# Two-layer float32 transformer chain on one core: mLSTM heads scored in pairs with the engines' orders changed, and eight low halves of weights made by GpSimd

## The chip, the cores and the metric

One NeuronCore of a Trainium2 chip runs the whole program. TensorE (PE) multiplies, VectorE (DVE) and ScalarE (ACT) do elementwise work, GpSimd (POOL) does a little of it and issues some transfers, SyncE (SP) issues the weight transfers. The metric is the device time of one execution in microseconds (us), lower is better.

## The reference

Activations of 256 tokens by 1024 features pass through two blocks of two layers each, all in float32. The two places that the change touches are the latent attention of the first layer and the mLSTM mixer of the last one:

```python
def _mla(x, positions, w_dq, q_norm, w_uq, w_dkv, kv_norm, w_ukv, w_o):
    cq = _rmsnorm(x @ w_dq, q_norm)
    q = (cq @ w_uq).reshape(b, s, h, MLA_NOPE + MLA_ROPE)      # 8 heads, 128 + 64
    q = jnp.concatenate([q[..., :MLA_NOPE], _rope(q[..., MLA_NOPE:], ...)], axis=-1)
    ckv = x @ w_dkv
    c_kv = _rmsnorm(ckv[..., :MLA_KV_LORA], kv_norm)
    k_pe = _rope(ckv[..., None, MLA_KV_LORA:], ...)
    kv = (c_kv @ w_ukv).reshape(b, s, h, MLA_NOPE + MLA_V)
    ...                                                          # causal softmax attention
    return o.reshape(b, s, h * MLA_V) @ w_o

def mlstm_mixer(u, b_gates, qk_conv_w, head_norm_g):             # 4 heads of 192
    qk, v, o_pre, gates = jnp.split(u, [2 * D_TOK, 3 * D_TOK, 4 * D_TOK], -1)
    qk = jax.nn.silu(causal_dwconv(qk, qk_conv_w))
    q, k = jnp.split(qk, 2, -1)
    ...
    # per head: sc = (q @ k.T) * w_intra ; num = sc @ v + inter-chunk state
    # den = sum(sc) + ... ; h = num / max(|den|, exp(-m))
    h = (h - mu) * lax.rsqrt(var + LN_EPS) * head_norm_g
    return jax.nn.sigmoid(o_pre) * h

def second_block(...):
    ...
        u = x @ w_in_mlstm[j]
        tok = mlstm_mixer(u[..., :4 * D_TOK + 2 * ML_HEADS], ...)
        xa = memory_cross_attention(u[..., -D_XA:], mem_kv)
        mix = jnp.concatenate([tok, xa], -1) @ w_out[l]
```

## The kernel before

**Weights in units.** Every weight matrix is cut into units of up to 128 x 2048 numbers, listed in the order of use (`order`). SyncE loads them in that order into six slots; a unit's slot comes free when TensorE has finished with the unit six places earlier. Each float32 number is used as two parts: ScalarE copies the loaded unit (`raw`) into a high half (`whi`, `split_hi`, L288), and a subtraction makes the low half (`wlo<-raw,whi`). VectorE makes the low half (`split_lo`, L299), in three cases GpSimd (`split_lo_gpsimd`, L293). TensorE then multiplies three times (`product`, L438): high by high, high by low, low by high. Before it uses a unit it waits for its low half (`wait_split`).

**Order by hand.** Each engine runs one list of instructions in the order written; nothing is reordered, and the engines meet only in semaphores. A `Splitter` makes the splits of all units in turn: `split.after(u)` makes those up to four units beyond u. Where such a call stands in an engine's list decides when that unit's half is made, and what waits behind it.

**Latent attention** (`mla_tensor`, `mla_scalar`, `mla_vector`, the first 78 us). Its units are numbered 0 to 12: 0 to 3 down projections, 4 to 6 the query projections (4 the rotary part `qp`, 5 and 6 the heads, `qn0` and `qn1`), 7 and 8 the key and value projections (`kn`, `v`), 9 to 12 the output projection. VectorE turns the rotary parts (`rotate`, L1223 to L1228) and normalises the latents (`roots`, a chain of small instructions at L424 to L430), then makes four low halves in a row (`split.after(qn1, 5)`: units 8 to 11), then the attention's maxima and divisions. TensorE transposes the normalised latents (`turn_latents`) before it can start on unit 6.

**mLSTM** (`ml_tensor`, `ml_scalar`, `ml_vector`, 1228 to 1368 us). Units: `VG` 0 to 3 (values and gates), `XQ` 4, `QK` 5 to 10 (queries and keys, two chunks of 128 channels each), `OU` 11 to 14 (output gate), `WO` 15 to 18 (output projection). A QK unit goes through TensorE (`qk_unit`), a first tap and a tanh on ScalarE, three taps and a gate on VectorE (`taps` L2244, `gate` L2260). Four heads of 192 channels lie over chunks of 128, so a head is one whole chunk and one half of another. `score(h)` (L2037) multiplies keys with queries, `masked` and `weights` make the decay weights, `weighted` (L2278) multiplies them in, `numerator` (L2053 to L2057) multiplies with the values, `divided` divides. `maxima` (L2025) spreads a row of maxima over the partitions. `cross1` is the cross attention to the memory, in steps between the others (L1676, L490, L1700). At the end VectorE normalises the heads and makes the tokens (`l_tok`), which TensorE transposes (`turn_tokens`) between pieces of `WO[0]`; `WO[1]` to `WO[3]` follow in `tail_tensor`.

Of the kernel before, what the change touches and what calls it, by code (L numbers as in the profile page):

```python
# [26 lines left out]
P = 128  # L27
# [21 lines left out]
def build(nc, a, out):  # L49
# [29 lines left out]
    with ctx:  # L79
# [286 lines left out]

        first_loaded = sem("first_loaded")
# [1584 lines left out]
        def num_bank(h):  # L1952
            return (3, 4, 5, 4)[h]

        def score_bank(h):
            return (7, 7, 7, 6)[h]

        def qk_needed(h):

            return (2, 4, 6, 6)[h]  # L1960
# [22 lines left out]
        def ml_tensor(pe):  # L1983
# [36 lines left out]
            def maxima(h):  # L2020
                if h < 2:
                    pe.wait_ge(L["l_gc"], 2)
                else:
                    pe.wait_ge(L["l_wd"], 2)
# [3 lines left out]
            def score(h):  # L2028
                pe.wait_ge(L["l_qkd"], qk_needed(h))
                if h in (1, 2):  # L2030
                    pe.wait_ge(L["l_scd"], h)
                if h == 3:
                    pe.wait_ge(L["l_wd"], 4)
                pieces = head_rows(h)
                for to, k0, q0 in ((slice(0, S), 0, 0), (slice(S, 3 * P), P, P)):
                    for n, (c, r) in enumerate(pieces):
                        m = nc.tensor.matmul(ps[:, score_bank(h), to], l_qk(TC + c)[r, 0, k0:k0 + P],  # L2037
                                             l_qk(c)[r, 0, q0:S], start=n == 0,
                                             stop=n == len(pieces) - 1, skip_group_check=True)
                m.then_inc(L["l_sT"], 1)  # L2040

            def numerator(h):
                pe.wait_ge(L["l_scd"], h + 1)
                if h == 1:
                    pe.wait_ge(L["l_conv"], TC)
                if h == 2:
                    pe.wait_ge(L["l_conv"], TC)
                if h == 3:
                    pe.wait_ge(L["l_hd"], 2)
# [38 lines left out]
            qk_unit(2)  # L2088
            maxima(0)
            maxima(1)  # L2090
            cross1.tensor(pe, 2)
            qk_unit(3)
            score(0)
            cross1.tensor(pe, 3)
            qk_unit(4)
            numerator(0)
            cross1.tensor(pe, 4)
            qk_unit(5, (0,))
            qk_unit(5, (1,))
            score(1)  # L2100
            maxima(2)
            pe.wait_ge(L["l_wd"], 2)
            maxima(3)
            for j, u in enumerate(OU):
                wait_split(pe, u)
                for t in range(TT):
                    if j == 0 and t == 0:
                        pe.wait_ge(cross1.low, cross1.PAIRS)
                    if j == 0 and t == 1:
                        pe.wait_ge(L["l_hd"], 1)  # L2110
# [3 lines left out]
                    if j == 2 and t == 0:  # L2114
                        numerator(2)
                        numerator(3)
                m.then_inc(w_done[u.slot], 1)
                if j == 0:
                    numerator(1)
                if j == 1:  # L2120
                    score(2)
                    score(3)
# [19 lines left out]
        def ml_scalar(act, link, split):  # L2142
# [55 lines left out]
            act.wait_ge(L["l_gc"], 2)  # L2198
            weights(0)
            weights(1)  # L2200
            first_tap(3)
            cross1.scalar(act, 3)
            tanh(2)
            split.after(QK[3])
            first_tap(4)
            cross1.scalar(act, 4)
            tanh(3)
            split.after(QK[4])
            tanh(4)
            first_tap(5)  # L2210
            weights(2)
            tanh(5)
            split.after(QK[5])
            weights(3)
# [22 lines left out]
        def ml_vector(dve, link, split):  # L2237
# [106 lines left out]
            split.after(QK[1])  # L2344
            cross1.vector(dve, link, 2)
            masked(0)
            masked(1)
            taps(2)
            gate(1)
            split.after(QK[2])  # L2350
            cross1.vector(dve, link, 3)
            weighted(0)
            taps(3)
            gate(2)
            cross1.vector(dve, link, 4)
            split.after(QK[3])
            taps(4)
            gate(3)
            divided(0)
            split.after(QK[4])  # L2360
            gate(4)
            taps(5)
            weighted(1)
            masked(2)
            masked(3)
            head_stats(0)
            gate(5)
            split.after(QK[5])
            divided(1)
# [317 lines left out]
```

## Time and profile before

| what | value |
|---|---|
| median of 3 runs | 1559.56 us (1559.52 to 1561.84) |
| profiled execution | 1563.72 us, its span 1561.9 us, mean granted TensorE clock 0.996 |
| TensorE matmul busy | 1546.5 us, 99% |
| VectorE, ScalarE, GpSimd busy | 1051.3, 770.1, 35.6 us |

The span is what the profiler saw between first and last instruction; the profiled execution's own time is 1.8 us more. Matmuls are pipelined and their ends modelled, so a busy TensorE can also be a slow one: the granted clock of a stretch must be read beside it.

### The profile page before, as it was taken

What the parts mean: (1) busy time and instruction counts of PE and PEld (TensorE: products, weight loads), DVE (VectorE), ACT (ScalarE), POOL (GpSimd) and SP (SyncE); (2) the same over time, 40 slices, a digit from 0 to 9 for tenths busy, and PEclk for the clock granted to TensorE, in tenths of its full rate; (3) what the DMA queues carried; (4) which work ended last, traced back from release to release, by engine and by line L of the source; (5) the groups of instructions that cost most, each with busy time, mean ns of one, the idle gap of its engine ahead of it and who ended that gap; (6) DMA issues with size and microseconds to landing.
All of it is one profiled execution on the core that took longest, in us unless ns stands there. A gap on an engine that the chain in (4) does not pass through costs nothing.

```text
span 1561.9 us, 20701 instructions
## 1 busy us (share of the span) xinstructions
PE 1546.5 (99%) x8610; PEld 1338.4 (86%) x8610; DVE 1051.3 (67%) x1270; ACT 770.1 (49%) x913; POOL 35.6 (2%) x86
## 2 busy tenths in 40 slices
PE   9999999999999999999999999999999999999997
PEld 9888888899888888888899888888888897888886
DVE  7866657768676666655777665576555877965556
ACT  5735434567353444545464354545445464454543
POOL 2000000000000000000100000010000100000000
PEclk9999999999999999999999999999999998999999
DMA  9365654743565656555463755547555562375551
GB/s 286 121 215 189 190 189 161 242 162 109 170 209 191 192 182 216 188 189 190 162 214 135 242 189 188 189 156 246 192 189 188 161 208 84 126 243 189 189 190 53
DMA packets 198356, 285.97 MB, mean 183 GB/s; under 512 B 9199, under 2 KB 166967, under 8 KB 198263
## 3 DMA queue, kind: packets, MB, share of 16 engines
q1 hardware_dynamic: 194663, 272.19, 53.3%
q0 software_dynamic: 3456, 11.94, 2.4%
q8 instruction: 68, 1.11, 0.3%
q10 hardware_dynamic: 144, 0.52, 0.1%
q14 instruction: 25, 0.20, 0.0%
HBM read 283.58 MB, written 1.05 MB: 182 GB/s over the span
## 4 chain that ended last, share of the span: by engine, by line
PE 95%; DVE 3%; ACT 1%; issue 1%; DMA 0%; DVEq 0%; ACTq 0%
PE ps L438 50%; PE ps L467 25%; PE ps L471 13%; PE ps L490 3%; DVE wlo L299 1%; PE ps L2037 1%; ACT whi L288 0%; PE ps L1456 0%; DVE arena L2244 0%; PE ps L1700 0%; DMA x<-in_x 0%; DVE x L566 0%; PE ps L1131 0%; PE ps L1123 0%; PE ps L1121 0%
## 5 line engine op out<-in xcount | busy, mean ns | idle before, releaser
L299 DVE TENSOR_TENSOR wlo<-raw,whi 128x2048 fp32r<-128x2048 f32 (+3 forms) x254 | 567.1, 2262 | 222.2 <-ACT whi L288 221.5
L288 ACT ACTIVATE whi<-raw 128x2048 fp32r<-128x2048 f32 (+3 forms) x260 | 480.3, 1884 | 19.2 <-DMA raw<-in_w_out 5.1
L438 PE MATMUL ps<-whi,yt 128*128 128x512 f32 (+1 forms) x1472 | 460.8, 386 | 0.5 <-DVE wlo L299 0.5
L467 PE MATMUL ps<-xt,whi 128*128 128x512 f32 x1728 | 432.3, 392 | 0.0
L467 PEld LDWEIGHTS ps<-xt,whi 128*128 128x128 f32 x1728 | 314.2, 189 | 59.0
L438 PEld LDWEIGHTS ps<-whi,yt 128*128 128x128 f32 x1472 | 274.8, 188 | 54.5 <-DVE wlo L299 0.9
L438 PE MATMUL ps<-wlo,yt 128*128 128x512 f32 (+1 forms) x736 | 283.8, 386 | 0.0
L471 PEld LDWEIGHTS ps<-xt,wlo 128*128 128x128 f32 x1728 | 235.7, 190 | 16.9
L471 PE MATMUL ps<-xt,wlo 128*128 128x256 f32 x1728 | 240.9, 282 | 0.0
L438 PE MATMUL ps<-whi,xt 128*128 128x512 f32 (+4 forms) x778 | 220.2, 361 | 0.9 <-DVE wlo L299 0.3
L777 ACT ACTIVATE arena<-ps 128x512 f32<-128x512 f32 x108 | 64.2, 594 | 279.8 <-PE ps L471 279.8
L438 PEld LDWEIGHTS ps<-whi,xt 128*128 128x128 f32 x778 | 140.3, 190 | 22.6 <-issue 1.6
L438 PEld LDWEIGHTS ps<-wlo,yt 128*128 128x128 f32 x736 | 138.6, 188 | 24.6
L810 DVE TENSOR_TENSOR arena<-arena,ps 128x512 f32<-128x512 f32 x108 | 73.9, 684 | 125.4 <-ACT arena L777 125.4
L438 PE MATMUL ps<-wlo,xt 128*128 128x512 f32 (+4 forms) x389 | 138.5, 356 | 0.0
L800 ACT ACTIVATE yt<-arena 128x512 fp32r<-128x512 f32 x76 | 48.2, 634 | 124.4 <-DVE arena L830 69.4
L438 PE MATMUL ps<-xt,whi 128*128 128x256 f32 x560 | 102.7, 285 | 0.3 <-DVE wlo L299 0.3
L438 PEld LDWEIGHTS ps<-xt,whi 128*128 128x128 f32 x560 | 87.3, 192 | 4.0 <-issue 3.4
L840 DVE TENSOR_TENSOR yt<-arena,yt 128x512 fp32r<-128x512 f32 x76 | 52.6, 693 | 53.2 <-ACT yt L800 53.2
L438 PEld LDWEIGHTS ps<-wlo,xt 128*128 128x128 f32 x389 | 73.9, 190 | 9.2
L438 PE MATMUL ps<-xt,wlo 128*128 128x256 f32 x280 | 79.2, 283 | 0.0
L525 ACT ACTIVATE xt<-ps 128x512 fp32r<-128x512 f32 x40 | 22.7, 597 | 90.5 <-PE ps L490 90.5
(248 smaller groups left out, 943.2 us busy)
## 6 DMA issues: line engine op xcount, KB each, us to landing
raw<-in_ffn_w_up SPq DMA_DIRECT2D x76, 1024.0 KB, 5.3
raw<-in_ffn_w_down SPq DMA_DIRECT2D x76, 1024.0 KB, 4.8
raw<-in_ffn_w_gate SPq DMA_DIRECT2D x44, 1024.0 KB, 5.3
raw<-in_diff_w_qkv SPq DMA_DIRECT2D x12, 1024.0 KB, 5.1
raw<-in_w_in_conv SPq DMA_DIRECT2D x10, 1024.0 KB, 5.2
raw<-in_w_out SPq DMA_DIRECT2D x8, 1024.0 KB, 4.8
raw<-in_w_in_mlstm SPq DMA_DIRECT2D x7, 1024.0 KB, 8.3
raw<-in_w_in_mlstm SPq DMA_DIRECT2D x8, 768.0 KB, 4.2
```

The source lines that it names most:

```text
L288: nc.scalar.activation(whi[:, u.slot, 0:u.size], raw[:, u.slot, 0:u.size], ACT.Copy).then_inc(w_hi[u.slot], 1)
L299: nc.vector.tensor_tensor(wlo[:, u.slot, 0:u.size], raw[:, u.slot, 0:u.size], whi[:, u.slot, 0:u.size].bitcast(F32), ALU.subtract).then_in ...
L438: m = nc.tensor.matmul(out_, p, q, start=first and n == 0, stop=last and n == 2, skip_group_check=True)
L467: nc.tensor.matmul(o.rearrange("p (a n) -> p a n", a=2), parts[c][0], xt2[:, :, c, :], start=c == 0, stop=False, skip_group_check=True)
L471: m = nc.tensor.matmul(o[:, S:2 * S], parts[c][1], xthi[:, c, :], start=False, stop=c == KC - 1, skip_group_check=True)
L490: return nc.tensor.transpose(o, i, ident[0:i.shape[0], 0:i.shape[0]])
L525: nc.scalar.activation(half_x(xthi, t, h), turn_view(n, t, h), ACT.Copy).then_inc(x_hi, 1)
L777: nc.scalar.activation(f_half(kind == "U" and f.gated), both_halves(f_bank(f, kind, s), 1), ACT.Copy).then_inc(f_part, 1)
L800: nc.scalar.activation(h_part(s, 0), f_view(1), ACT.Copy).then_inc(f_hi, 1)
L810: nc.vector.tensor_tensor(f_half(2 + (kind == "U" and f.gated)), f_half(kind == "U" and f.gated), both_halves(f_bank(f, kind, s), 0), ALU. ...
L840: nc.vector.tensor_tensor(h_part(s, 1), f_view(1), h_part(s, 0).bitcast(F32), ALU.subtract).then_inc(f_lo, 1)
L2037: m = nc.tensor.matmul(ps[:, score_bank(h), to], l_qk(TC + c)[r, 0, k0:k0 + P], l_qk(c)[r, 0, q0:S], start=n == 0, stop=n == len(pieces) - ...
```

## The change

In the mLSTM stage, heads are scored two at a time (`scores(h)` for heads h and h + 1 into two banks). The whole chunk of the first head comes first, then the two halves of the shared chunk, alternating between the heads, then the whole chunk of the second. The two pairs now stand within unit `QK[5]` and within `OU[1]`; all engines' lists are rearranged around that, some banks change, and the mask products stand between halves of other units. VectorE makes no low half for eight units; GpSimd makes them: units 4, 6, 9, 10, 11, 12 of latent attention, and `WO[1]` and `WO[2]` of mLSTM.

```diff
         def split_lo(dve, u):
+            if u in pool_low:
+                return
             dve.wait_ge(w_hi[u.slot], u.use)
...
+        pool_low = [mla_u[k] for k in (4, 6, 9, 10, 11, 12)] + [ml_u[k] for k in (16, 17)]
...
         def num_bank(h):
-            return (3, 4, 5, 4)[h]
+            return (5, 4, 5, 4)[h]
         def score_bank(h):
-            return (7, 7, 7, 6)[h]
+            return 7 - h % 2
...
-            def score(h):
+            def scores(h):
                 pe.wait_ge(L["l_qkd"], qk_needed(h))
-                if h in (1, 2):
-                    pe.wait_ge(L["l_scd"], h)
-                if h == 3:
-                    pe.wait_ge(L["l_wd"], 4)
-                pieces = head_rows(h)
-                for to, k0, q0 in ((slice(0, S), 0, 0), (slice(S, 3 * P), P, P)):
-                    for n, (c, r) in enumerate(pieces):
-                        m = nc.tensor.matmul(ps[:, score_bank(h), to], l_qk(TC + c)[r, 0, k0:k0 + P],
-                                             l_qk(c)[r, 0, q0:S], start=n == 0,
-                                             stop=n == len(pieces) - 1, skip_group_check=True)
+                pe.wait_ge(L["l_wd"], h + 2)
+                if h:
+                    pe.wait_ge(L["l_scd"], 1)
+                (whole0, shared0), (shared1, whole1) = head_rows(h), head_rows(h + 1)
+                spans = ((slice(0, S), 0, 0), (slice(S, 3 * P), P, P))
+                def piece(g, part, span, first):
+                    (c, r), (to, k0, q0) = part, span
+                    return nc.tensor.matmul(ps[:, score_bank(g), to], l_qk(TC + c)[r, 0, k0:k0 + P],
+                                            l_qk(c)[r, 0, q0:S], start=first and span is spans[0],
+                                            stop=not first, skip_group_check=True)
+                for span in spans:
+                    piece(h, whole0, span, True)
+                for span in spans:
+                    m = piece(h, shared0, span, False)
+                    piece(h + 1, shared1, span, True)
+                m.then_inc(L["l_sT"], 1)
+                for span in spans:
+                    m = piece(h + 1, whole1, span, False)
                 m.then_inc(L["l_sT"], 1)
...
         def _(pool):
             start_gpsimd(pool)
+            for k in (4, 6):
+                split_lo_gpsimd(pool, mla_u[k])
             wait_high(pool, mla_u[8])
             load_gb(pool, 0)
+            for k in (9, 10, 11, 12):
+                split_lo_gpsimd(pool, mla_u[k])
             pool.wait_ge(m_ylo, KC)
...
+                    for k in (16, 17):
+                        split_lo_gpsimd(pool, ml_u[k])
```

**GpSimd in latent attention.** In the list of GpSimd before, these rows follow the making of the constants (`gb` takes a layer norm's gains and shifts, the row with `in_mem` the memory tokens):

```order
L2444 AFFINE_SELECT mtril<-mtril 128x128
L2446 AFFINE_SELECT sel<-sel 4x512
L594 DMA gb<-in_ln_mix_g 128x1024 [waits w_hi2]
L594 DMA gb<-in_ln_mix_b 128x1024
L2612 DMA arena<-in_mem 128x2x1024 [waits m_ylo]
L594 DMA gb<-in_ln_ffn_g 128x1024 [waits ln_x]
```

In the changed kernel the same place reads:

```order
L2454 AFFINE_SELECT sel<-sel 4x512
L293 TENSOR_TENSOR wlo<-raw,whi 128x1536 [waits w_hi4]
L293 TENSOR_TENSOR wlo<-raw,whi 128x1536 [waits w_hi0]
L597 DMA gb<-in_ln_mix_g 128x1024 [waits w_hi2]
L597 DMA gb<-in_ln_mix_b 128x1024
L293 TENSOR_TENSOR wlo<-raw,whi 128x2048 [waits w_hi3]
L293 TENSOR_TENSOR wlo<-raw,whi 128x2048 [waits w_hi4]
L293 TENSOR_TENSOR wlo<-raw,whi 128x2048 [waits w_hi5]
L293 TENSOR_TENSOR wlo<-raw,whi 128x2048 [waits w_hi0]
L2624 DMA arena<-in_mem 128x2x1024 [waits m_ylo]
```

Six subtractions now stand here, for units 4 and 6 ahead of the first gains and for units 9 to 12 behind them, each waiting only for its high half.

**VectorE in latent attention.** This is VectorE's list before, from the end of the rotation of the queries (second half of the tokens) to the first maxima of the attention:

```order
L1227 TENSOR_TENSOR res<-ps,rope_m 128x512
L1228 TENSOR_TENSOR res<-res,arena 128x512 [waits dve_step]
L299 TENSOR_TENSOR wlo<-raw,whi 128x2048 [waits w_hi2,m_qpe]
L299 TENSOR_TENSOR wlo<-raw,whi 128x2048 [waits w_hi3]
L299 TENSOR_TENSOR wlo<-raw,whi 128x2048 [waits w_hi4]
L299 TENSOR_TENSOR wlo<-raw,whi 128x2048 [waits w_hi5]
L1286 COPY arena<-ps 128x512 [waits m_v0] x2
L936 TENSOR_TENSOR ps<-ps,masks 128x256 [waits mla_scored]
L940 TENSOR_REDUCE small<-ps 128x1 [waits dve_step]
```

In the changed kernel it reads:

```order
L1230 TENSOR_TENSOR res<-ps,rope_m 128x512
L1231 TENSOR_TENSOR res<-res,arena 128x512 [waits dve_step]
L301 TENSOR_TENSOR wlo<-raw,whi 128x2048 [waits w_hi2,m_qpe]
L1289 COPY arena<-ps 128x512 [waits m_v0] x2
L939 TENSOR_TENSOR ps<-ps,masks 128x256 [waits mla_scored]
L943 TENSOR_REDUCE small<-ps 128x1 [waits dve_step]
```

Of the four low halves in a row only that of unit 8 is left, between an addition with two operands in SBUF and the copies of the values; the low half of unit 6 is gone from a place 11 rows further up.

**TensorE in mLSTM.** Before, from unit `QK[3]` to `QK[4]` (`ps<-yf` is a score, `ps<-ident,arena` and `ps<-arena,kvm` the cross attention, `128x193` a numerator; the "..." stands for the unit's other products):

```order
L438 MATMUL ps<-xt,whi 128x256 [waits l_conv,w_lo2]
...
L2037 MATMUL ps<-yf 128x256 [waits l_qkd]
L2037 MATMUL ps<-yf 128x256
L2037 MATMUL ps<-yf 128x128 x2
L490 MATMUL ps<-ident,arena 128x128 [waits cross1_copied,cross1_normed]
L1700 MATMUL ps<-arena,kvm 64x256 [waits cross1_exped,cross1_copied]
L438 MATMUL ps<-xt,whi 128x256 [waits l_conv,w_lo3]
...
L2053 MATMUL ps<-arena 128x193 [waits l_scd]
L1700 MATMUL ps<-arena,kvm 64x256 [waits cross1_copied]
```

In the changed kernel, from `QK[3]` to the scores within `QK[5]`:

```order
L441 MATMUL ps<-xt,whi 128x256 [waits l_conv,w_lo2]
...
L493 MATMUL ps<-ident,arena 128x128 [waits cross1_copied,cross1_normed]
L1703 MATMUL ps<-arena,kvm 64x256 [waits cross1_exped,cross1_copied]
L441 MATMUL ps<-xt,whi 128x256 [waits l_conv,w_lo3]
...
L1703 MATMUL ps<-arena,kvm 64x256 [waits cross1_copied]
L441 MATMUL ps<-xt,whi 128x256 [waits l_conv,w_lo4]
...
L2041 MATMUL ps<-yf 128x256 [waits l_wd,l_qkd]
L2041 MATMUL ps<-yf 128x128
L2041 MATMUL ps<-yf 128x256 x2
L2041 MATMUL ps<-yf 128x128 x2
```

No score stands behind `QK[3]` any more; the first pair comes after the first half of `QK[5]`, and nothing between asks for `l_qkd` or `l_scd`, which VectorE's gates and weighted scores raise.

## Rows read from the trace of the kernel before

**Rows 1.** TensorE's waits, whole kernel: us in total, times, longest us.

```profile
PE ps L2037 <- DVE yf L2260: 2.3, 1, 2.3
...
PE ps L438 <- DVE wlo L299: 1.0, 3, 0.5
```

**Rows 2.** A window of mLSTM: length, PE busy, PEclk, DMA share, GB/s.

```profile
1295.30:1302.10 6.80, 6.80 (x25) 0.51 0.16 63
```

**Rows 3.** Timeline of TensorE, mLSTM: start, us, what [idle before].

```profile
1294.93 3.33 PE L2037 MATMUL ps<-yf 128*128 128x256 f32 x8 [2.27 <-DVE yf L2260]
...
1316.00 2.16 PE L2037 MATMUL ps<-yf 64*128 64x256 f32 x8
...
1330.15 3.74 PE L2037 MATMUL ps<-yf 128*128 128x256 f32 x16
```

**Rows 4.** The chain that ended last, mLSTM: start, us, what.

```profile
1319.22 5.92 PE ps L438 x24
...
1326.12 4.20 PE ps L438 x24
```

**Rows 5.** Windows of latent attention: columns as in the window above.

```profile
57.00:62.00 5.00, 4.40 (x33) 1.00 0.68 210
71.00:79.00 8.00, 7.32 (x40) 1.00 0.01 2
```

**Rows 6.** Timeline of GpSimd: its first low half, end of a feed-forward stage.

```profile
769.25 4.91 POOL L293 TENSOR_TENSOR wlo<-raw,whi 128x2048 fp32r<-128x2048 f32 x1 [168.01 <-ACT whi L288]
```

**Rows 7.** Timeline of VectorE around the GpSimd row above.

```profile
767.40 2.29 DVE L299 TENSOR_TENSOR wlo<-raw,whi 128x2048 fp32r<-128x2048 f32 x1 [1.18 <-ACT whi L288]
769.61 0.68 DVE L541 SCALAR_TENSOR_TENSOR res<-x,ps 128x512 f32<-128x512 f32 x1
...
772.73 1.99 DVE L559 SCALAR_TENSOR_TENSOR res<-res,mv,gb 128x512 f32<-128x512 f32 x1
...
776.01 0.75 DVE L559 SCALAR_TENSOR_TENSOR res<-res,mv,gb 128x512 f32<-128x512 f32 x1
```

**Rows 8.** The same at GpSimd's second low half: GpSimd, then VectorE.

```profile
1043.18 4.91 POOL L293 TENSOR_TENSOR wlo<-raw,whi 128x2048 fp32r<-128x2048 f32 x1 [168.05 <-ACT whi L288]
...
1046.65 1.98 DVE L559 SCALAR_TENSOR_TENSOR res<-res,mv,gb 128x512 f32<-128x512 f32 x1
```

**Rows 9.** Timeline of VectorE in latent attention.

```profile
29.47 0.19 DVE L2573 TENSOR_SCALAR rope_m<-ang 128x64 f32<-128x64 f32 x1
...
35.09 1.75 DVE L299 TENSOR_TENSOR wlo<-raw,whi 128x1536 fp32r<-128x1536 f32 x1
...
42.24 0.69 DVE L1228 TENSOR_TENSOR res<-res,arena 128x512 f32<-128x512 f32 x1
...
45.14 8.90 DVE L299 TENSOR_TENSOR wlo<-raw,whi 128x2048 fp32r<-128x2048 f32 x4
```

**Rows 10.** Timeline of ScalarE in latent attention: the high halves.

```profile
27.56 3.55 ACT L288 ACTIVATE whi<-raw 128x1536 fp32r<-128x1536 f32 x2
...
37.97 3.75 ACT L288 ACTIVATE whi<-raw 128x2048 fp32r<-128x2048 f32 x2
...
42.53 3.76 ACT L288 ACTIVATE whi<-raw 128x2048 fp32r<-128x2048 f32 x2
```

**Rows 11.** Timeline of TensorE: the starts of units 6 and 8.

```profile
36.89 0.50 PE L438 MATMUL ps<-xt,whi 128*128 128x256 f32 x2 [0.25 <-DVE wlo L299]
...
47.49 0.50 PE L438 MATMUL ps<-whi,xt 128*128 128x512 f32 x1 [0.27 <-DVE wlo L299]
```

**Rows 12.** Timeline of ScalarE, end of mLSTM: high halves of WO[0] to WO[2].

```profile
1326.51 5.50 ACT L288 ACTIVATE whi<-raw 128x2048 fp32r<-128x2048 f32 x3
```

**Rows 13.** Timeline, end of mLSTM: VectorE's third division to first tokens.

```profile
1337.01 0.16 DVE L2287 COPY small<-ps 128x2 f32<-128x2 f32 x1 [0.32 <-PE ps L2057]
...
1346.39 0.96 DVE L2398 SCALAR_TENSOR_TENSOR res<-res,arena 128x768 f32<-128x768 f32 x1
```

**Rows 14.** Timeline of TensorE: the transposes of the first tokens.

```profile
1348.29 0.81 PE L490 MATMUL ps<-ident,res 128*128 128x128 f32 x6
```

More of the change, by code:

```diff
@@ L2043, in numerator @@
                 pe.wait_ge(L["l_scd"], h + 1)
[L2044 to L2049, printed above, removed]
+                if h < 2:
+                    pe.wait_ge(L["l_conv"], TC - 1 + h)
+                else:
+                    pe.wait_ge(L["l_hd"], h - 1)
                 b = ps[:, num_bank(h), :]
@@ L2092, in ml_tensor @@
             qk_unit(3)
-            score(0)
             cross1.tensor(pe, 3)
             qk_unit(4)
-            numerator(0)
             cross1.tensor(pe, 4)
             qk_unit(5, (0,))
+            scores(0)
             qk_unit(5, (1,))
[L2100 to L2103, printed above, removed]
             for j, u in enumerate(OU):
@@ L2113, in ml_tensor @@
                         m.then_inc(L["l_o0"], 1)
-                    if j == 2 and t == 0:
-                        numerator(2)
-                        numerator(3)
+                    if j == 0 and t == 0:
+                        maxima(2)
+                        maxima(3)
+                    if j == 1 and t == 0:
+                        scores(2)
                 m.then_inc(w_done[u.slot], 1)
                 if j == 0:
+                    numerator(0)
                     numerator(1)
                 if j == 1:
-                    score(2)
-                    score(3)
+                    numerator(2)
+                    numerator(3)
             wait_split(pe, WO[0])
@@ L2204, in ml_scalar @@
             split.after(QK[3])
+            tanh(3)
             first_tap(4)
             cross1.scalar(act, 4)
-            tanh(3)
+            tanh(4)
             split.after(QK[4])
-            tanh(4)
             first_tap(5)
-            weights(2)
             tanh(5)
             split.after(QK[5])
+            weights(2)
             weights(3)
@@ L2343, in ml_vector @@
             gate(0)
-            split.after(QK[1])
             cross1.vector(dve, link, 2)
+            taps(2)
+            gate(1)
             masked(0)
             masked(1)
-            taps(2)
-            gate(1)
-            split.after(QK[2])
+            split.after(QK[1])
             cross1.vector(dve, link, 3)
-            weighted(0)
             taps(3)
             gate(2)
+            gate(3)
+            split.after(QK[2])
+            taps(4)
             cross1.vector(dve, link, 4)
+            gate(4)
+            weighted(0)
+            weighted(1)
             split.after(QK[3])
[L2357 to L2361, printed above, removed]
             taps(5)
-            weighted(1)
+            gate(5)
             masked(2)
             masked(3)
+            split.after(QK[4])
+            divided(0)
+            divided(1)
+            weighted(2)
+            weighted(3)
+            split.after(QK[5])
             head_stats(0)
-            gate(5)
-            split.after(QK[5])
-            divided(1)
             head_stats(1)
             split.after(OU[0])
-            weighted(2)
-            weighted(3)
             split.after(OU[1])
```

11 lines of the change are left out of this document (5 added, 6 removed).

## The prediction

> **What bounds the kernel now.** TensorE is busy 99% of the span by the table above, so only four things change the time: its idle time, its clock, the work it has, and new waits. I read its waits first [rows 1]: over the whole kernel the largest is one of 2.3 us for a gate of mLSTM, and low halves from VectorE cost 1.0 us in three places. Then the clock. Right after that wait TensorE runs 6.8 us at a mean granted clock of 0.51 [rows 2], that is at 1.2 GHz in place of 2.4; before it fell the engine had stood idle 2.27 us [rows 3]. Later, the first output-gate unit takes 5.92 us where the next, with the same 24 records, takes 4.20 [rows 4]. Latent attention runs at full clock, with idle time of 0.60 and 0.68 us in two windows [rows 5]. Outside these two stages there is nothing that the change could touch: TensorE is busy throughout and its list there is the same.
>
> **mLSTM, TensorE's own list.** The score behind `QK[3]`, which waited, is gone from there; the first pair stands 12 us of other work later. That removes the wait, 2.3 us. The slow stretch costs 6.8 x 0.49 = 3.3 us, the slow unit 5.92 - 4.20 = 1.7 us. Scores: two in a row at full clock take 3.74 us for 16 records [rows 3]. Of a pair's 8 products the 4 on the shared chunk use rows 0 to 63 and 64 to 127 alternately, into different banks. If two such run at once a pair costs 6/8 of 3.74, 2.8 us, so both pairs save 1.9, and the second score alone took 0.3 more than its share (2.16). I take 2.0 us in all (0.3 if nothing overlaps). `maxima(0)` now stands in the middle of `QK[2]` and may wait about 0.2 us for ScalarE's gate columns. The low half of `WO[2]` costs 0.5 us before [rows 1] and would be made on GpSimd in time. Together: -2.3 - 3.3 - 1.7 - 2.0 - 0.5 + 0.2 = -9.6 us. This half of the change is good by itself.
>
> **What GpSimd's low halves do to VectorE.** The trace of before has three low halves on GpSimd. One takes 4.91 us from 769.25, so to 774.16 [rows 6]. VectorE's layer-norm instruction L559 (`res<-res,mv,gb`, two tensors from SBUF) starts at 772.73 in it and takes 1.99 us in place of 0.75; it ends 0.56 us after GpSimd does. The L541 beside it, which reads one tensor from PSUM, takes its usual 0.68 [rows 7]. At the second low half, 1043.18 to 1048.09, the same instruction takes 1.98 us and ends 0.54 us after GpSimd [rows 8]. So an instruction of VectorE with two SBUF operands stands still until GpSimd's subtraction is done. The other way round it waits as well: GpSimd's row begins 0.44 us before VectorE's split (767.40 + 2.29) is over [rows 6, 7], so I count 4.5 us for a 128x2048 low half and 3.4 us for 1536.
>
> The Trainium skill says the same (SBUF — State Buffer, "Who interferes with whom"): a VectorE instruction with two SBUF inputs, or in a two-port mode, contends with a GpSimd instruction that reads SBUF, and whoever issues first holds the shared ports for the whole instruction. By that rule the trace agrees, with the 1.99 us. Its page GPSIMD Engine Reference ("Elementwise — side-by-side cycle accounting") gives 4497 ns for a 2048-wide float32 tensor_tensor; with 4.91 us in its place the sum below would be about 3 us longer.
>
> **Latent attention with that price.** I walk the lists.
> (a) Unit 6: its high half ends at 27.56 + 1.5 = 29.1 [rows 10]. GpSimd then works to 32.5, while VectorE stands in the small table and root instructions that precede the latents' transposes. From L2573 to the old place of unit 6's split it needs 35.09 - 29.47 = 5.6 us [rows 9], now from 32.5: 38.1. TensorE needs 0.35 us more for three transposes and starts unit 6 at 38.45 in place of 36.89 [rows 11]: +1.6. If the small instructions pass until the roots (some 1.3 us further), it is +0.7.
> (b) Everything hanging on these transposes moves with them. Unit 9's high half was done at 41.72, 0.5 us before VectorE's first L1228 (`res<-res,arena`, two SBUF operands, 42.24) [rows 9, 10]; both move 1.6, to 43.25 and 43.8. So GpSimd begins unit 9 first and VectorE waits to 47.75, then adds to 48.45. Unit 10 goes to 52.95; the second L1228 waits for it, to 53.6. It raises a semaphore for which unit 8's split waits, and in that gap unit 11, which has waited longer, begins: to 58.1. Only then comes unit 8's low half, 8.90/4 = 2.25 us, to 60.35. TensorE wanted it at 48.8 and starts at 60.5 in place of 47.49 [rows 11]: +13.0, (a) included. If VectorE gets in before unit 11, it is 4.5 less, +8.5.
> (c) TensorE idles some 11 us there; before, 2.27 us were enough for the lower clock. The price is between 1.7 and 3.3 us; dense products follow, as in the case of 1.7, which I take.
> (d) Three low halves less before the attention free VectorE there: the idle 0.60 and 0.68 us go, -1.3.
> (e) Unit 12 falls beside the attention's first divisions: GpSimd's 4.5 us against TensorE's lead of some 3.5: +1.0 (0 to 3).
> Sum: +13.0 + 1.7 - 1.3 + 1.0 = +14.4 us. Units 4, 9 to 12 themselves are not late: TensorE needs unit 9 over 10 us after GpSimd has it. The memory transfer behind them waits for the attention's end as before.
>
> **mLSTM with that price.** ScalarE's high halves of `WO` follow the last `weights`, at 1326.51 before, 1.83 us each [rows 12], and some 9 us earlier now: `WO[1]` is ready near 1321.2. GpSimd works from there to 1325.8; VectorE's split of `OU[3]`, due near 1323, waits 2.9 us and ends at 1327.6. `WO[2]` then runs to 1332.1, and VectorE's split of `WO[0]`, due at 1329.0, waits 3.1. These 6.0 us go into the chain to the tokens, 10.3 us from the third division [rows 13]. Before, it ended 0.9 us ahead of TensorE's transposes (1347.35, 1348.29) [rows 13, 14]. With TensorE 9.6 us earlier and VectorE about as much without the waits, that lead is used up. So +6.0, and a spell at the lower clock, +1.7: mLSTM gives -9.6 + 7.7 = -1.9.
>
> **Sum:** +14.4 - 1.9 = +12.5 us. The profiled execution took 1563.7, so 1576.2 in its like; the median of the runs is 4.2 us lower, and 1559.6 + 12.5 = 1572.1 us.
>
> **Rivals.** Within 0.2% (3.1 us) of before counts as no change.
> *Faster: the blocking is rare.* It was seen on one form, at 512 columns. If long subtractions on both engines share SBUF, or GpSimd comes second in most meetings, -9.6 in mLSTM and -1.3 and -0.5 (waits for units 6 and 8) in latent attention remain: 1548. It decides at (b): should VectorE's first L1228 begin before unit 9, the queue of three never forms. For it: only 0.5 us separates them. Against: both hang on the same transposes, so (a) does not change their order. 0.2.
> *Milder: VectorE wins each contested hand-over.* (b) is +8.5, (e) 0, mLSTM as above: +8.9 - 1.9 = +7, 1566.5. 0.15.
> *No change: both halves cancel,* with blocking as in the milder case but short waits in mLSTM (-6): about 1560. 0.08.
> *The scores do not overlap and the clock falls anyway.* +1.7 and up to +5 on the forecast, 1575 to 1579. Inside the forecast's range.
> My forecast has 0.57, with 1565 to 1579 as its own range. The low end is (a) at 0.7 and a part of the hand-overs, the high end 4.91 us a piece and 3.3 for the clock. The whole range, 1552 to 1580, reaches into the faster case. Faster 0.2, same 0.08, slower 0.72.
>
> **What the new profile would show.** (1) GpSimd L293 rows at 43 to 58 us nearly without gaps, and VectorE's L1231 and the split behind it lasting 4 to 5 us. (2) A wait of TensorE of 7 to 12 us for `wlo`, L301, near 49, and granted clock 0.5 behind it. (3) In mLSTM no wait for `yf`, full clock from 1290 to 1325 in old time, pairs of scores near 2.8 us. (4) A wait of TensorE for `res` (the tokens) of about 6 us. I am wrong if the rows of (1) keep their old lengths.

## The result, and the profile after

The changed kernel takes 1576.08 us (median of 4 runs, 1575.41 to 1576.41) against 1560.6 for the kernel before in the same measurement (4 runs, 1559.52 to 1561.84): the ratio is 1.0093, with a 95% interval of 1.008 to 1.0106. It is 15.5 us slower; 1572.1 was forecast. Its profiled execution took 1575.94 us, with a span of 1574.1, 12.2 more than that of before.

TensorE's waits in the changed kernel (us in total, times, longest), which answer to [rows 1]:

```profile
PE ps L441 <- DVE wlo L301: 10.3, 1, 10.3
PE ps L493 <- DVE res L2406: 5.5, 1, 5.5
PE ps L493 <- DVE res L1269: 2.2, 2, 1.6
PE ps L493 <- DVE arena L993: 1.5, 2, 1.1
```

The 2.3 us for `yf` are gone. In their place stand 10.3 us for one low half and 5.5 us for the tokens. The first is unit 8's, in latent attention. GpSimd (first row) and VectorE there, in the timeline of the changed kernel:

```profile
44.67 14.48 POOL L293 TENSOR_TENSOR wlo<-raw,whi 128x2048 fp32r<-128x2048 f32 x3 [0.53 <-ACT whi L288]
```

```profile
44.33 0.68 DVE L1230 TENSOR_TENSOR res<-ps,rope_m 128x512 f32<-128x512 f32 x1
45.05 4.81 DVE L1231 TENSOR_TENSOR res<-res,arena 128x512 f32<-128x512 f32 x1
...
50.56 0.68 DVE L1230 TENSOR_TENSOR res<-ps,rope_m 128x512 f32<-128x512 f32 x1
51.28 3.52 DVE L1231 TENSOR_TENSOR res<-res,arena 128x512 f32<-128x512 f32 x1
54.89 6.41 DVE L301 TENSOR_TENSOR wlo<-raw,whi 128x2048 fp32r<-128x2048 f32 x1
```

Three subtractions of GpSimd run from 44.67 to 59.15 without a gap. L1230, with one operand from PSUM, keeps its 0.68 us in the middle of them; L1231, with both from SBUF, takes 4.81 and 3.52, and unit 8's split 6.41 in place of 2.25. It ends at 61.30, and TensorE starts on the unit at 61.35, 13.9 us later than before [rows 11] (0.4 us of that is the start-up: the split that VectorE begins at 27.08 us in the profile of before begins at 27.49 here, and at 27.61 in a second profile of before). What its clock does around that (each row a stretch, then its length, TensorE's busy time with its records, granted clock, DMA share and GB/s):

```profile
36.00:38.00 2.00, 0.43 (x5) 1.00 0.71 174
38.00:40.00 2.00, 1.40 (x8) 0.68 0.87 342
40.00:42.00 2.00, 2.00 (x11) 0.50 0.38 152
42.00:44.00 2.00, 2.00 (x18) 0.97 0.00 0
...
61.00:63.00 2.00, 1.65 (x4) 0.50 0.00 0
63.00:65.00 2.00, 2.00 (x8) 0.50 0.00 0
65.00:67.00 2.00, 2.00 (x10) 0.74 0.00 0
```

There are two spells at 1.2 GHz: one after the 1.57 and 0.60 us of idle time at the latents, one after the long wait. Over 34 to 90 us TensorE idles 14.1 us in place of 1.8 and loses 3.9 us to the lower clock (busy time times the missing share of the clock, summed over windows of 2 us); in the same stretch of before it loses nothing. Together 16.2 us. GpSimd's transfer of the memory tokens, which waits for the attention's end, says the same; first the changed kernel:

```profile
95.63 0.76 POOL L2624 DMA_DIRECT2D arena<-in_mem  x1 [20.54 <-DVE yt L1161]
```

Before it stands at 79.42:

```profile
79.42 0.72 POOL L2612 DMA_DIRECT2D arena<-in_mem  x1 [38.08 <-DVE yt L1158]
```

In mLSTM the chain of waits of the changed kernel reads (start, us, what):

```profile
1321.05 2.36 PE ps L2041 x16
...
1335.79 2.37 PE ps L2041 x16
...
1338.66 4.62 DVE wlo L301
...
1344.54 5.38 DVE wlo L301
...
1359.19 0.97 DVE res L2406
...
1360.20 1.54 PE ps L493 x6
```

A pair of scores takes 2.4 us on this chain. The splits of `OU[3]` and `WO[0]` take 4.62 and 5.38 us, 2.9 and 3.1 more than their own 1.75 and 2.24, and the chain from them to the tokens makes TensorE wait 5.5 us. Its clock is down behind that wait too: the windows 1359 to 1361, 1361 to 1363 and 1363 to 1365 us have granted 0.67, 0.50 and 0.98, which costs 1.3 us, reckoned as above. From 1270 to 1350 us it is at 1.00. The stage, taken from the gains' transfer behind one layer norm to that behind the next, is 126.2 us (1261.25 to 1387.40); in the profile of before it is 130.2 (1245.06 to 1375.22). So 16.2 us were lost in latent attention and 4.0 won in mLSTM: 12.2, the difference of the spans.

### The profile page after: what moved, and what is told of

Same layout as the page of the kernel before. It is cut to its first block, busy times and chain, and to the rows that moved or that the text cites. A ratio compares the mean times of both kernels' runs of the same rounds, so it can differ in the third digit from the quotient of the medians.

```text
span 1574.1 us, 20699 instructions
## 1 busy us (share of the span) xinstructions
PE 1543.1 (98%) x8610; PEld 1339.2 (85%) x8610; DVE 1057.7 (67%) x1262; ACT 769.5 (49%) x913; POOL 72.9 (5%) x94
## 4 chain that ended last, share of the span: by engine, by line
PE 93%; DVE 5%; DMA 1%; issue 1%; ACT 0%; SPq 0%; DVEq 0%; ACTq 0%
PE ps L441 49%; PE ps L470 25%; PE ps L474 13%; PE ps L493 3%; DVE wlo L301 1%; DMA raw<-in_mla_w_dkv 1%; DVE res L1231 1%; PE ps L1459 0%; PE ps L2041 0%; PE ps L1679 0%; PE ps L1124 0%; PE ps L1703 0%; PE ps L1134 0%; PE ps L1126 0%; DVE x L569 0%
## 5 line engine op out<-in xcount | busy, mean ns | idle before, releaser
L301 DVE TENSOR_TENSOR wlo<-raw,whi 128x2048 fp32r<-128x2048 f32 (+2 forms) x246 | 560.4, 2307 | 223.3 <-ACT whi L288 222.8
L441 PE MATMUL ps<-whi,xt 128*128 128x512 f32 (+4 forms) x778 | 220.0, 360 | 10.9 <-DVE wlo L301 10.3
L293 POOL TENSOR_TENSOR wlo<-raw,whi 128x2048 fp32r<-128x2048 f32 (+2 forms) x11 | 50.3, 4580 | 603.7 <-ACT whi L288 603.7
```

The source lines that it names most:

```text
L293: nc.gpsimd.tensor_tensor(wlo[:, u.slot, 0:u.size], raw[:, u.slot, 0:u.size], whi[:, u.slot, 0:u.size].bitcast(F32), ALU.subtract).then_in ...
L441: m = nc.tensor.matmul(out_, p, q, start=first and n == 0, stop=last and n == 2, skip_group_check=True)
```

## The experiments

**The parts of the change.** Four kernels were compared with one another and with the kernel before (1562.3 us there, 15 runs).

*The order alone*, and *its mLSTM halves*: in the first `pool_low` is empty and GpSimd's new calls are gone, in the second only `WO[1]` and `WO[2]` remain.

```diff
-        pool_low = [mla_u[k] for k in (4, 6, 9, 10, 11, 12)] + [ml_u[k] for k in (16, 17)]
+        pool_low = []                                # order alone
+        pool_low = [ml_u[k] for k in (16, 17)]       # with the mLSTM halves
```

> The mLSTM order alone; VectorE makes all low halves as before. Theory (the order is worth about 10 us and GpSimd's subtractions cost everything else): 1550 to 1552 us, 9 to 10 us below before; latent attention reads like before (its first memory transfer at 79.4 us), no wait of TensorE for yf in mLSTM, WO[2]'s wait of 0.5 us may stay. Rival (GpSimd's halves free VectorE and the order is worth less): 1556 us or more, and waits for wlo in mLSTM.

> The new order, with only WO[1] and WO[2] on GpSimd. Theory: their blocking of VectorE ahead of the tokens costs 6 to 8 us, so 1556 to 1558 us against about 1550 of the order alone, with TensorE's wait of about 5.5 us for res (the tokens). Rival (TensorE would wait for the tokens anyway, because its own list is now shorter): 1550 to 1552 us, the same as the order alone, and a wait of about 5 us for res in both.

Measured: the order alone 1556.56 us, ratio 0.9965 (0.9952 to 0.9977), so 5.7 us faster than before and not 9 to 10. The time is the rival's, but its waits for low halves are not there (1.0 us over the whole kernel, as before). With the mLSTM halves 1560.47, ratio 0.9991 (0.9982 to 1.0), 3.9 us above the order alone. TensorE's first wait in each, the order alone first:

```profile
PE ps L493 <- DVE res L2406: 1.6, 1, 1.6
```

```profile
PE ps L493 <- DVE res L2406: 5.5, 1, 5.5
```

Neither theory had it whole. The shorter list of TensorE makes it wait for the tokens anyway, 1.6 us; the blocking adds 3.9 us to that wait. The blocking is there in the splits, which take 4.62 and 5.46 us with the mLSTM halves, 6.1 us above their own time; but VectorE is also rid of `WO[1]`'s split of 2.24 us, which stands ahead of the tokens in the order alone, and 6.1 - 2.2 is 3.9. That the medians differ by 3.9 us too is in part chance: behind the longer wait the profile with the mLSTM halves has granted 0.50 over 1344 to 1348 us, 1.9 us lost, that of the order alone has none, and their spans differ by 5.1 us (1558.7 and 1553.6).

*The six halves of latent attention on the order of before.*

> The order of before, with the six low halves of latent attention on GpSimd. Theory: the latent attention of the changed kernel is reproduced, 16 us longer, so 1575 to 1577 us, with TensorE's wait of about 10 us for unit 8. Rival (the orders of mLSTM and the halves interact, or the profiled 16 us are partly given back later): 1570 us or less.

Measured: 1577.61 us, ratio 1.0104 (1.0088 to 1.0119), +15.3 us. TensorE waits 9.9 us for unit 8, and 1.6 and 0.6 us at the latents as in the changed kernel. The cost is all in this part, and none of it is given back. The parts add up: -5.7 + 3.9 + 15.3 = 13.5 us, and the changed kernel is 13.8 us above the 1562.3.

*The shared chunk not alternating*, on the order alone:

```diff
                 for span in spans:
                     m = piece(h, shared0, span, False)
+                for span in spans:
                     piece(h + 1, shared1, span, True)
```

> The order alone, but the shared chunk's products run as both spans of the first head and then both of the second, in place of alternating. Theory (alternating row halves into different banks run at once): a pair of scores takes 3.1 to 3.7 us in place of 2.4, so the kernel is 1.5 to 2.5 us above the order alone. Rival (the pair is short because of the full clock and the missing gap, or adjacent products overlap in any order): within 0.5 us of the order alone.

Measured: 1556.1 us, ratio 0.996 (0.9948 to 0.9973). The chain of waits of this kernel has the pairs at

```profile
1304.93 2.37 PE ps L2041 x16
```

and again at 1319.67 with 2.38 us, the same 2.4 us. So alternating is worth nothing over one head's half products behind the other's. That fells the theory's forecast, but not what it rests on, that products on rows 0 to 63 and 64 to 127 run at once: the other half of the rival, that they overlap in any order, stands, and the trace shows it. A product has two records here. In a stretch of 0.03 us of this kernel's timeline (1305.80 to 1305.83) TensorE has

```profile
1305.51 0.49 PE L2041 MATMUL ps<-yf 64*128 64x256 f32 x2
```

two half products, one of each head, that started 0.013 us apart. All four half products take 0.86 us (1305.51 to 1306.37), the two whole ones ahead of them 0.75 (1304.77 to 1305.51). In the changed kernel the same view has the two at once as well:

```profile
1321.64 0.49 PE L2041 MATMUL ps<-yf 64*128 64x256 f32 x2
```

**What blocks VectorE.** Four more, beside 1563.21 us for the kernel before (15 runs).

*Units 9 to 12 behind unit 8.*

```diff
             load_gb(pool, 0)
+            pool.wait_ge(w_lo[mla_u[8].slot], 2 * mla_u[8].use)
             for k in (9, 10, 11, 12):
```

> The changed kernel, but GpSimd begins units 9 to 12 only when VectorE has made unit 8's low half. Theory (the 10.3 us are VectorE standing in turn behind three subtractions of GpSimd): the wait for unit 8 falls to 0 to 2 us, L1231 and L301 take their own 0.7 and 2.2 us there, and the kernel is 8 to 12 us below the changed one, 1564 to 1568 us; unit 12 comes later (after 66 us) and may cost 0 to 3 us of that. Rival (the delay lies in units 4 and 6 and in the small instructions before the latents): less than 4 us gained.

Measured: 1571.41 us, ratio 1.0055 (1.0042 to 1.0068), 4.7 us below the changed kernel's 1576.08 and not 8 to 12. TensorE's longest wait in it and, in its timeline, VectorE and GpSimd:

```profile
PE ps L493 <- DVE arena L993: 6.3, 1, 6.3
```

```profile
48.01 2.29 DVE L301 TENSOR_TENSOR wlo<-raw,whi 128x2048 fp32r<-128x2048 f32 x1
...
60.92 7.73 DVE L993 TENSOR_SCALAR arena<-arena,small 128x128 f32<-128x128 f32 x2
```

```profile
50.44 18.06 POOL L293 TENSOR_TENSOR wlo<-raw,whi 128x2048 fp32r<-128x2048 f32 x4 [6.25 <-DVE wlo L301]
```

Unit 8's split takes its own 2.29 us, and nobody waits for it: the queue of three was the cause of the 10.3 us. But the four subtractions now lie beside the attention, whose first division L993 stands still until the last ends at 68.50. Moving GpSimd's work moves the collision. L993 has one tensor from SBUF, so two such operands are not the only thing that is blocked.

*Quarters.* Each subtraction of GpSimd in four instructions (the three that GpSimd made before, too):

```diff
-            nc.gpsimd.tensor_tensor(wlo[:, u.slot, 0:u.size], raw[:, u.slot, 0:u.size],
-                                    whi[:, u.slot, 0:u.size].bitcast(F32),
-                                    ALU.subtract).then_inc(w_lo[u.slot], 2)
+            n = u.size // 4
+            for k in range(4):
+                m = nc.gpsimd.tensor_tensor(wlo[:, u.slot, k * n:k * n + n], ...)
+            m.then_inc(w_lo[u.slot], 2)
```

> The changed kernel with each of GpSimd's subtractions cut in four of 512 or 384 columns, one behind the other (the three of before too). Theory (whoever holds the shared ports keeps them for one instruction): a blocked instruction of VectorE waits 1.1 us at most, so the wait for unit 8 is below 5 us and the one for the tokens below 4, and the kernel is 6 to 12 us below the changed one. Rival (GpSimd's whole queue keeps VectorE out, since its next instruction follows without a gap): within 2 us of the changed kernel, a wait of about 10 us again.

Measured: 1564.54 us, ratio 1.0016 (1.0007 to 1.0026), 11.5 us below the changed kernel. The wait for unit 8 is 2.8 us; that for the tokens 4.3, a little over what was expected. In its timeline:

```profile
45.38 1.40 DVE L1235 TENSOR_TENSOR res<-res,arena 128x512 f32<-128x512 f32 x1
...
48.20 1.54 DVE L1235 TENSOR_TENSOR res<-res,arena 128x512 f32<-128x512 f32 x1
49.83 3.19 DVE L305 TENSOR_TENSOR wlo<-raw,whi 128x2048 fp32r<-128x2048 f32 x1
```

L1235 is L1231 of the changed kernel: 1.4 and 1.5 us in place of 4.81 and 3.52. The blocking lasts one instruction, and VectorE gets in behind it even when GpSimd's next instruction waits for nothing. GpSimd pays: its last 16 quarters, four units, take 22.87 us against 18.06 for four whole ones. A quarter with nothing beside it takes 1.24 us, start to start, so 16 would take 19.9; the other 3 us are three turns that VectorE had. What the low halves on GpSimd cost is read against the order alone (1556.56 us): 19.5 us whole, 8.0 in quarters.

*Reading against writing.* VectorE makes all low halves; GpSimd does work of its own at the eight places, on a tensor that nobody reads, each instruction waiting for the one before: two subtractions of half a unit, or four writes of zeros.

```diff
+            for _ in range(2):
+                own(nc.gpsimd.tensor_tensor(scratch[:, 0:u.size // 2], scratch[:, 0:u.size // 2],
+                                            scratch[:, 0:u.size // 2], ALU.subtract))
```

```diff
+            for _ in range(4):
+                own(nc.gpsimd.memset(scratch[:, 0:u.size // 2], 0.0))
```

> The new order with VectorE making all low halves; at the eight places GpSimd makes, in place of each low half, two subtractions of half its size on a tensor of its own, which nobody reads. Theory (reading SBUF on GpSimd blocks VectorE's two-operand instructions, whatever the data): a wait of TensorE for unit 8 of 5 us or more, as VectorE now has its own low halves to make besides, and 12 us or more above the order alone (1568 us or more). Rival (the waits come from the data: units 9 to 12 and the semaphores on them): within 2 us of the order alone, 1555 to 1559 us.

> The same, but GpSimd writes zeros in place of subtracting: four writes of half a unit's columns at each of the eight places. Theory (only an instruction of GpSimd that reads SBUF blocks VectorE): 1555 to 1559 us, VectorE's split of 2048 columns takes 2.25 us beside it. Rival (any work of GpSimd on SBUF blocks): longer by as much as the private subtractions, in proportion to how long the writes last; VectorE's splits beside them take over 3 us.

Measured: with the subtractions 1573.09 us, ratio 1.0062 (1.005 to 1.0075), 16.5 us above the order alone; with the writes 1556.54, ratio 0.9959 (0.9945 to 0.9973), the time of the order alone. VectorE's four splits in a row of latent attention, beside the subtractions:

```profile
50.82 13.99 DVE L308 TENSOR_TENSOR wlo<-raw,whi 128x2048 fp32r<-128x2048 f32 x4
```

and beside the writes, with GpSimd's row:

```profile
45.63 8.90 DVE L307 TENSOR_TENSOR wlo<-raw,whi 128x2048 fp32r<-128x2048 f32 x4
```

```profile
47.62 8.03 POOL L301 MEMSET scratch<- 128x1024 f32 x8 [1.54 <-ACT whi L289]
```

8.90 us is what they take with GpSimd idle [rows 9]. So it is neither the data, nor the semaphores of the low halves, nor GpSimd's being busy. What the subtraction has and the write has not is that it reads, beside computing; an instruction of GpSimd that only reads was not run. The wait for unit 8 of 5 us that I expected beside the subtractions did not come; they began later there, and TensorE waited at the latents (2.1 us), for ScalarE's part of the attention (3.1, L984 there) and for the tokens (5.4). Writing is not harmless to every instruction, however. Beside writes of 0.8 us from 29.13 to 32.26, the same timeline has

```profile
29.08 0.84 DVE L2584 TENSOR_SCALAR ang<-ang 128x80 f32<-128x80 f32 x1
29.96 0.76 DVE L2587 COPY rope_m<-ang 128x64 f32<-128x64 f32 x1
```

where these two take 0.20 us in the profile of before. With the copy of the changed kernel beside unit 6's subtraction,

```profile
29.67 3.49 DVE L2579 COPY rope_m<-ang 128x64 f32<-128x64 f32 x1
```

there are two kinds of victims: two SBUF operands stand still beside reading, and copies and operations with a scalar from SBUF to SBUF beside reading and writing (one of a single column, L555 in the changed kernel, keeps its 0.15 us beside a subtraction). The Trainium skill (SBUF — State Buffer, "Who interferes with whom") says both, and names such copies and `tensor_scalar` as the forms that have a two-port mode; the 0.84, 0.76 and 3.49 us agree.

**What was left open.** Four more, beside 1562.73 us for the kernel before (27 runs).

*The order of products within a head*, on the order alone:

```diff
                 for span in spans:
                     piece(h, whole0, span, True)
-                for span in spans:
                     m = piece(h, shared0, span, False)
-                    piece(h + 1, shared1, span, True)
                 m.then_inc(L["l_sT"], 1)
                 for span in spans:
+                    piece(h + 1, shared1, span, True)
                     m = piece(h + 1, whole1, span, False)
```

> The order alone, with the pairs kept, but each head's products in the sequence of before: for each span first the whole chunk (128 rows), then the half (64 rows). Theory formed from the last runs (what a score costs beyond its columns is the change between 128 and 64 rows at every product; nothing runs at once): a pair takes 3.5 us again in place of 2.4, 1.1 us for each pair, 2 us in all. Rival (the pair is short because two heads stand together in two banks): 2.4 us a pair.

Measured: 1558.44 us, ratio 0.9975 (0.9965 to 0.9984), 2.2 us above the 1556.25 of the order alone with `WO[1]` moved (below), on the same chip. Its timeline:

```profile
1305.10 3.74 PE L2041 MATMUL ps<-yf 128*128 128x256 f32 x16
```

3.74 us, exactly as in [rows 3], and 2.52 for the grouped pair in the same view; from the first record to the next instruction a pair takes 3.49 us here and 2.28 grouped, 1.2 us less. The expectation came true in its number, but its "nothing runs at once" did not: two things differ between the sequences. This one has 6 changes between 128 and 64 rows in a pair, the grouped one 2. And here only the last half product of the first head and the first of the second are neighbours and run at once; the others stand alone, as in the timeline of 1305.75 to 1305.90:

```profile
1305.63 0.48 PE L2041 MATMUL ps<-yf 64*128 64x256 f32 x1
```

So one more product of 256 columns has to be done by itself, 0.43 us by the starts of such products (0.22 and 0.21 us from record to record). The other 0.8 us are four changes, 0.20 us each. The starts say so directly: around a change they lie 0.31 and 0.32 us apart. The Trainium skill (TensorEngine Tiling (Array Packing), "Key Properties") says that a change of tiling mode, not of tile, drains the engine; by that rule the trace agrees, with this 0.20 us. The page lets different tiles work in parallel too; the trace agrees, with half products that start 0.007 us (alternating) and 0.013 us (one head behind the other) apart.

*The kernel before, unchanged, once more.*

> The kernel before, unchanged, for a second profile of it. Theory (the lower clock behind the wait for yf, and the slow first output-gate unit, differ from one execution to the next): the stretch at half clock is nearer 4 us than 7, the output-gate unit takes 4.2 us, and the span is 2 to 3 us shorter than the 1561.9 of the first profile. Rival (both belong to the kernel): 1561 to 1562 again. The ratio says what no change at all looks like in this measurement.

Measured: 1562.42 us (12 runs), ratio 1.0001 (0.9993 to 1.001), span 1559.4. The clock, in this second profile:

```profile
1297.00:1299.00 2.00, 2.00 (x11) 0.60 0.04 8
1299.00:1301.00 2.00, 2.00 (x11) 0.55 0.00 0
1301.00:1303.00 2.00, 2.00 (x18) 1.00 0.00 0
...
1310.00:1320.00 10.00, 10.00 (x65) 1.00 0.46 165
1320.00:1330.00 10.00, 10.00 (x58) 1.00 0.40 125
```

and in the first profile of before, for the output-gate unit:

```profile
1318.00:1319.00 1.00, 1.00 (x6) 1.00 1.03 406
1319.00:1320.00 1.00, 1.00 (x4) 0.68 0.99 397
1320.00:1322.00 2.00, 2.00 (x7) 0.50 0.22 88
1322.00:1323.00 1.00, 1.00 (x7) 0.61 0.00 0
```

The wait of 2.27 us is the same, the spell behind it costs 1.7 us in place of 3.3, and the spell at the output-gate unit, which no idle time precedes, is absent: the unit takes 4.42 us in place of 5.92. The runs show it as well. Of 69 runs of the kernel before, the 7 with a mean granted clock of 0.999 over the span took 1559.2 to 1560.0 us, the 15 with 0.998 took 1560.8 to 1561.7, the 46 with 0.996 or 0.997 took 1562.0 to 1565.9, and one with 0.995 took 1564.6. The median of all is 1562.5. Two thirds of the runs have a mean clock like the first profile's, so losses of its size are no rarity; with two profiles it is open how often each spell comes.

*`WO[1]`'s low half behind the tokens*, on the order alone:

```diff
             split.after(OU[0])
-            split.after(OU[1])
             divided(2)
```

> The order alone, with WO[1]'s low half made by VectorE behind the tokens in place of ahead of the third division. Theory (VectorE has no idle time from 1318 us to the tokens, but its work behind them is as urgent): the wait for the tokens goes (-1.6 us) and one for WO[1] and WO[2] of about 2 us comes, within 0.5 us of the order alone. Rival (only the tokens are urgent): 1.5 us below it, 1554 to 1555 us.

Measured: 1556.25 us, ratio 0.9959 (0.9947 to 0.9971), as the order alone. TensorE's first wait in it is

```profile
PE ps L441 <- DVE yt L2411: 1.7, 1, 1.7
```

1.7 us for the low half of the tokens in place of 1.6 for the tokens. VectorE is the bound in this stretch, and moving its work within it gains nothing.

*Units 4 and 6 alone on GpSimd*, on the order of before.

> The kernel before with only units 4 and 6 of latent attention on GpSimd. Theory (the small table instructions stand still beside unit 6, and the latents come late): unit 6 starts 1.5 us late, TensorE waits 1.6 and 0.6 us for res (L1269's place), a spell of lower clock follows, and the kernel is 1.5 to 3.5 us above before. Rival (freeing VectorE of two splits pays for it): within 1 us of before.

Measured: 1565.54 us, ratio 1.0015 (1.0004 to 1.0026), 2.8 us above before. TensorE waits 1.54 and 0.59 us at the latents, and 40 to 44 us are at a granted clock of 0.66 and 0.50.

```profile
39.28 0.52 PE L493 MATMUL ps<-ident,res 128*128 128x128 f32 x3 [1.54 <-DVE res L1269]
40.40 0.71 PE L493 MATMUL ps<-ident,res 128*128 128x128 f32 x3 [0.59 <-DVE res L1269]
```

## Why the prediction was right, point by point

The forecast (1572.1, slower) was right in its sign, in its mechanism and, in the terms of the two profiles, in its sum: +12.5 against +12.2. That the sum agrees so well is in part luck: latent attention was put 1.8 us too low and mLSTM 2.1 us too high. The base was off as well.

**The lock**, its main step, held: rows of both kernels, the quarters, and the pair of subtractions and writes show it apart from the other causes that were named. The rival "the blocking is rare" fell, with that of the milder hand-over: VectorE did not get in before unit 11.

**(b) Unit 8** came out row by row. GpSimd first, L1231 behind unit 9, the second L1231 behind unit 10, unit 11 ahead of the split: forecast 60.35 for the low half, measured 61.30, mostly since GpSimd began unit 9 at 44.67 and not 43.25. The delay is 13.9 us for 13.0. The quarters and the hand-over say how the turn is decided: as far as the rows tell, whoever already waits when the other's instruction ends goes next. At 54.8 VectorE had just ended an instruction and its split still waited for a semaphore, while unit 11 waited for the ports.

**(a) Unit 6** had its mechanism right (the first copy waits 3.49 us), but it was priced too low. TensorE starts on the unit at 39.63, 2.7 us later than before for 1.6, 0.4 of it from the start-up. And a part of the price was missing: the 1.57 and 0.60 us of idle time bring a spell of the lower clock of their own, 1.5 us in the windows above (0.68, 0.50 and 0.97). Units 4 and 6 alone, for which 1.6 was forecast, cost 2.8 us.

**(c) to (e)** gave +1.4 in the forecast. What is left of the stage's 16.2 us behind the 13.9 is 2.3, the clock behind the long wait, so (d) and (e) together came to nothing: in place of the idle 1.3 us stand the waits for L993, 1.5 us. Latent attention was mis-sized by 1.8 us.

**mLSTM's own list**, -9.6 us, was the term with the largest error against the medians: the order alone gives -5.7. Three parts of it were wrong:
- The slow stretch and the slow unit, 3.3 + 1.7 us, were taken from one profile. In the second profile of the same kernel they come to 1.7 + 0.2 (4.42 against 4.20). A spell of lower clock is no fixed property of a place in the list.
- The tokens: I had VectorE's lead used up only with the blocking, but the order alone already makes TensorE wait 1.6 us.
- The scores save 3.1 us, not 2.0 (2.1 + 2.1 + 3.5 us to the next instruction in the second profile of before, 2 x 2.28 now). Half products run at once, as forecast, but that gives only some 1.1 us: two of the eight in the pair of [rows 3] did so before, so 6/8 of its 3.74 us was not the measure. The other 2.0 us are ten changes between 128 and 64 rows fewer (14 before, 4 now, 0.20 us each), which the forecast did not know. The pair takes 2.52 us in the measure in which it said 2.8.
In the second profile of before these make up the gain: -2.3 for `yf`, -1.9 for the clock, -3.1 for the scores, +1.6 for the tokens is -5.7 us, and the spans differ by 5.8 (1559.4 to 1553.6).

**mLSTM with the lock**, +6.0 + 1.7: the two splits wait 2.9 and 3.1 us and the lower clock follows the wait (1.3 us) as forecast, but the step left out that VectorE is rid of `WO[1]`'s 2.24 us on the same chain. Measured by the medians, +3.9. By the medians, then, too large a gain and too large a loss cancel: -5.7 + 3.9 = -1.8 for the -1.9 of the forecast, which is luck. By the profiles it is -4.0, since the first profile of before has both its spells to lose: -2.3 for `yf`, -5.0 for the clock, -3.1 for the scores and -0.5 for `WO[2]`, then +5.5 for the tokens and +1.3 for the clock behind them, is -4.1.

**The base.** I took the profiled execution as 4.2 us above the typical run. It is nearly typical: 1563.72 against 1562.5 over 69 runs, and the median of three runs that I had, 1559.56, has two at 1559.5 us, where of the 69 only executions at a mean clock of 0.999 lie. With 1562.5 as its base the same sum gives 1575.0, so 2.9 of the 4.0 us between forecast and result are the base. Against 1562.5 the change costs 13.6 us; against the 1560.6 of its own measurement, 15.5.

Of the four signs that the new profile was to show, (1), (2) and (4) came as said (10.3 and 5.5 us; the rows of (1) last 3.5 to 6.4 us). Of (3), the full clock and the missing wait came, with pairs of 2.5 us and not 2.8.

## What to carry to other kernels

Before work moves from a busy VectorE to an idle GpSimd, walk through VectorE's instructions that will lie beside it. Those with two SBUF operands, and copies and operations with a scalar from SBUF to SBUF, stand still until GpSimd's instruction ends, so what counts is its longest instruction, not its busy share (5% here); on this kernel the four fastest versions measured (1556.1 to 1556.6 us) move no low half to GpSimd. If the work must go there, cut it in pieces: quarters gave back 11.5 of the 19.5 us that it cost. Matrix products of unlike row counts belong grouped, and products on the two halves of the rows next to one another. And a spell of lower clock in one profile should be looked for in a second one, and the base taken from more than three runs, before either enters a sum in full.

## What the runs showed of the hardware beyond that

- The change between products of 128 and of 64 rows costs 0.20 us, worked out from two forms of the same 8 products (16 records). Float32 products on rows 0 to 63 and 64 to 127 into different banks run at once when they stand together in the list, alternating or two and two: four take 0.86 us, two whole ones of the same columns 0.75.
- TensorE fell to 1.2 GHz at 1319.4 us in one profile of the kernel before with no idle time ahead of it, behind four small products of 4 rows and 256 columns; in the second profile of the same kernel, behind the same products, it did not. The profile of the kernel with units 4 and 6 on GpSimd has the slow spell too (0.83 over 1320 to 1330).
- GpSimd's writes of 768 columns, 0.8 us each, hold up a copy of 64 columns for 0.6 us, while the subtractions of 2048 columns with two SBUF operands beside them take no longer than alone.
- With the subtractions in quarters, both engines take turns instruction by instruction. Four copies of the rotary table, 0.20 us each before, take 0.94 to 1.06 us there, one quarter each.
